# Low halves a unit later, output banks held out of the round, the values' activation right behind the taps

## The reference

```
x, 256 x 1024
first block
  h = rmsnorm(x);  proj = h @ w_in                       (1024 x 3592)
  mixer 1: q, k, v of 4 heads of 128 through a causal convolution of 4 taps and silu,
           then the gated delta rule in chunks of 64 (a triangular solve per chunk and a scan),
           rmsnorm, times silu(z)
           and differential attention, 4 heads, two maps each: softmax a - lam * softmax b
  x = x + [rule, attention] @ w_out
  x = x + (silu(gate) * up) @ w_down,  d_ff 2816;  final rmsnorm
second block
  mod = silu(c) @ w_ada + b_ada                          (1024 x 6144, one row)
  mixer 2: attention of 8 heads of 64 with a relative bias, and glu -> depthwise convolution
           of 31 taps -> layer norm -> silu; both projected, gated and mixed by w_mix_o
  x = x + (gelu(gate) * value) @ w_down, with a convolution of 3 taps ahead of the gelu
```

## Time and profile before

| | us |
|---|---|
| median of 3 runs (794.73 to 796.6) | 796.13 |
| the profiled execution | 794.25 |
| its span, first to last instruction | 792.4 |
| TensorE busy | 754.2 (95%) |
| VectorE busy | 575.6 (73%) |
| ScalarE busy | 390.8 (49%) |
| GpSimd busy | 27.8 (4%) |
| mean granted TensorE clock | 0.988 of full |

### The profile page before, as it was taken

One profiled execution on the slowest core, in us unless ns is written; L12 is line 12 of the kernel. 1 busy time (PEld: TensorE's weight loads), 2 busy tenths in 40 slices (PEclk: granted clock), 3 DMA queues, 4 the chain that ended last, 5 costly groups with the idle time before them and its releaser, 6 DMA issues.

```text
span 792.4 us, 13350 instructions
## 1 busy us (share of the span) xinstructions
PE 754.2 (95%) x5290; PEld 694.6 (88%) x5290; DVE 575.6 (73%) x963; ACT 390.8 (49%) x661; POOL 27.8 (4%) x32
## 2 busy tenths in 40 slices
PE   7998999678999999999999989999999999999996
PEld 7987999677799999999979987799979899999995
DVE  5748888655665867768668998867766766766776
ACT  5472222644543534434565434458256655655644
POOL 0030000010000000000013000000000000000000
PEclk9999999889999999999999999999999999999999
DMA  7834444432279888789815632354444665465531
GB/s 289 281 94 157 134 160 159 157 110 81 80 242 403 324 299 285 271 282 335 306 55 186 212 108 73 114 213 142 155 157 135 212 196 202 161 193 204 161 134 53
DMA packets 40526, 148.94 MB, mean 188 GB/s; under 512 B 4496, under 2 KB 4624, under 8 KB 40080
## 3 DMA queue, kind: packets, MB, share of 16 engines
q1 hardware_dynamic: 39600, 142.91, 52.5%
q10 hardware_dynamic: 864, 5.18, 1.7%
HBM read 147.02 MB, written 1.05 MB: 187 GB/s over the span
## 4 chain that ended last, share of the span: by engine, by line
PE 76%; DVE 12%; ACT 7%; issue 3%; DMA 1%; POOL 0%; DVEq 0%; SPq 0%; ACTq 0%
PE bank L1014 13%; PE bank L1017 13%; PE bank L1015 13%; PE bank L1055 6%; PE bank L1053 6%; PE bank L1056 6%; PE bank L1031 5%; PE bank L1180 5%; DVE wlo L1410 3%; PE bank L1044 3%; DVE arena L1416 3%; ACT whi L1956 2%; ACT arena L1956 2%; DVE arena L1410 2%; ACT XN L1956 1%
## 5 line engine op out<-in xcount | busy, mean ns | idle before, releaser
L1014 PE MATMUL bank<-hh,whi 128*128 128x256 f32 x1008 | 289.6, 287 | 0.8 <-DVE hl L1410 0.5
L1015 PE MATMUL bank<-hl,whi 128*128 128x256 f32 x1008 | 285.9, 284 | 0.0
L1017 PE MATMUL bank<-hh,wlo 128*128 128x256 f32 x1008 | 285.8, 284 | 0.0
L1410 DVE TENSOR_TENSOR wlo<-raw,whi 128x1024 fp32r<-128x1024 f32 x202 | 243.1, 1236 | 48.6 <-ACT whi L1956 48.5
L1956 ACT ACTIVATE whi<-raw 128x1024 fp32r<-128x1024 f32 x202 | 202.4, 1047 | 27.9 <-DMA raw<-w_dram 20.0
L1014 PEld LDWEIGHTS bank<-hh,whi 128*128 128x128 f32 x1008 | 194.0, 192 | 5.0 <-issue 2.9
L1015 PEld LDWEIGHTS bank<-hl,whi 128*128 128x128 f32 x1008 | 193.9, 192 | 1.5
L1017 PEld LDWEIGHTS bank<-hh,wlo 128*128 128x128 f32 x1008 | 193.9, 192 | 0.0
L1416 DVE SCALAR_TENSOR_TENSOR arena<-bank,cols,arena 128x255 f32<-128x255 f32 (+3 forms) x138 | 58.9, 480 | 33.6 <-ACT arena L1956 31.8
L1956 ACT ACTIVATE arena<-bank 128x256 f32<-128x256 f32 (+2 forms) x65 | 26.9, 422 | 96.3 <-PE bank L1017 71.2
L1055 PE MATMUL bank<-wlo,fh 128*128 128x512 f32 x176 | 69.2, 393 | 1.1 <-DVE wlo L1410 1.1
(11 more groups left out here) (169 smaller groups left out, 888.6 us busy)
## 6 DMA issues: line engine op xcount, KB each, us to landing
raw<-w_dram SPq DMA_DIRECT2D x268, 512.0 KB, 4.7
arena<-rows_dram ACTq DMA_DIRECT2D x1, 1792.0 KB, 10.2
X<-x_dram SPq DMA_DIRECT2D x2, 512.0 KB, 4.3
arena<-rows_dram ACTq DMA_DIRECT2D x1, 1024.0 KB, 13.6
arena<-bias_dram ACTq DMA_DIRECT2D x1, 1024.0 KB, 16.9
out_dram<-X SPq DMA_DIRECT2D x4, 256.0 KB, 2.0
const<-const_dram ACTq DMA_DIRECT2D x1, 640.0 KB, 3.8
arena<-bias_dram ACTq DMA_DIRECT2D x1, 512.0 KB, 6.1
```

The costliest lines, as they stand in the source:

```text
L1014: e.matmul(o, a, hh[:, k, :], start=(k == 0), stop=False)
L1015: e.matmul(o, a, hl[:, k, :], start=False, stop=False)
L1017: ins = e.matmul(o, wlo[:, s, k * 128:k * 128 + 128], hh[:, k, :], start=False, stop=(k == 7))
L1410: return e.tensor_tensor(out, a, b, op)
```

## The change

Six edits:
1. In the early stream two a units fewer per early main unit: the sixteen of them follow main units 16 to 27 (two behind 18, 20, 22 and 24), where they followed 14 to 27 (two behind 19 and 23).
2. `prepare` splits in two steps. `hi` (ScalarE) is placed at once; `prep` (VectorE's low half or ada product, SyncE's fetch) is placed one call later while `lag` is on, that is during the turns of both mixers.
3. `silu` 2 follows directly on conv 10. The flag that lets `vturn` go is set one turn sooner, and `delta` has one turn more ahead of it, so that `vturn` keeps its place.
4. The banks of o0 and o1 are taken with a hold, dropped when `la_rows` 1 is placed; `silu` 3 moves from behind `turn_la` to ahead of `la_rows` 1.
5. `turn1` 4 goes ahead of `scores1` 5.
6. The two subtractions ident - Ym move on VectorE from `lev_first` to the end of `lev_mask`.

```diff
@@ stream
-        for _ in range((14 <= n < 28) + (n in (19, 23))):
+        for _ in range((16 <= n < 28) + (n in (18, 20, 22, 24))):
@@ Plan
+        self.lag, self.late = False, []
     def prepare(self, last):
+        new = []
         while self.prepared <= last:
...
                 self.lo_on[i] = (sem, self.lo_count[sem])
+                self.step("hi", i)
+            new.append(i)
+            self.prepared += 1
+        for i in self.late + ([] if self.lag else new):
             self.step("prep", i)
-            self.prepared += 1
+        self.late = new if self.lag else []
@@ main1
             P.step("conv", f)
+            if f == 10:
+                P.step("silu", 2)
             yield
-        last = qk(3)
-        next(last)
-        yield
-        P.step("silu", 2)
         flags.add("v")
-        yield from last
+        yield from qk(3)
@@ delta
         while "v" not in flags:
             yield
+        yield
...
-        P.fill("o0")
+        held = [P.take(hold=True)]
+        P.fill("o0", held[0])
         P.step("values_la", 0)
...
-        P.fill("o1")
+        held.append(P.take(hold=True))
+        P.fill("o1", held[1])
         P.step("values_la", 1)
         P.step("la_rows", 0)
         yield
         P.step("la_sums", 1)
         yield
-        P.step("la_rows", 1)
-        yield
         while "s7" not in flags or ("z", 0) not in flags:
             yield
+        P.step("silu", 3)
+        P.step("la_rows", 1)
+        P.held.difference_update(held)
+        yield
         held = P.take(hold=True)
         P.fill("oT0")
         P.fill("oT1", held)
         P.step("turn_la")
-        P.step("silu", 3)
@@ attention1
+                if n == 5:
+                    P.fill(f"pt1{n - 1}")
+                    P.step("turn1", n - 1)
                 for m in range(2):
                     P.fill(f"s1{n}{m}")
...
-            if n:
+            if n and n != 5:
                 P.fill(f"pt1{n - 1}")
@@ both mixers
+    P.lag = True
     turns(...)
+    P.lag = False
@@ VectorE
-            def lev_first():
                 for b in range(2):
                     w.wait_ge("ym", b + 1)
                     tt(Um[:, b, :, :], rep(K("ident"), 4), Ym[:, b, :, :], ALU.subtract).then_inc(sems["um0"], 1)
+
+            def lev_first():
@@ ScalarE
-            def prep(i):
-                if i in place:
-                    ...
+            def hi(i):
+                ...
```

More of the change, by code:

```diff
@@ L1959, in start @@
                 e.dma_start(const[:, 0, :], const_d[:, 0, :]).then_inc(sems["const"], 16)
-            def prep(i):
-                if i in place:
[L1963 to L1967, removed]
+            def hi(i):
+                s, n = place[i] % HL, place[i]
+                w.wait_ge(*fetched(i))
+                if n >= HL:
+                    w.wait_ge(*P.done[P.split[n - HL]])
+                af(whi[:, s, :], raw[:, i % RAW, :], ACT.Copy).then_inc(sems["hi"], 1)
             def sumsq(q):
@@ L2273, in _ @@
             does = {
-                "start": start, "prep": prep, "square": sumsq, "squares": sumsq, "sumsq": sumsq, "root": root, "rows": rows, "tv": tv, "th": th, "split_ba": split_ba,
+                "start": start, "hi": hi, "square": sumsq, "squares": sumsq, "sumsq": sumsq, "root": root, "rows": rows, "tv": tv, "th": th, "split_ba": split_ba,
                 "conv": conv, "silu": silu, "lam": lam_, "vd": vd_, "qk": qk, "z": z, "gates": gates, "dsq": dsq, "decay": decay,
```

## The result

The changed kernel takes 786.36 us (median of 4 runs, 786.13 to 787.85) beside 795.86 for the kernel before (4 runs, 794.73 to 796.6). The ratio is 0.9886, interval 0.9868 to 0.9903: 1.1% faster. The forecast was 785.2, in a range of 778.5 to 792.5.

The account below looks back on a forecast made before the run. TensorE bounds the kernel, so time lies only in its waits and the low clock behind them. Terms 4.1 + 4.3 + 1.8 - 0.8 + 1.5 = 10.9 us off 794.25 give 783.3, median 785.2, range 778.5 to 792.5.

Parts of the forecast that it names:

- Part 1: First mixer, before the first level: later low halves and moved ada units shorten TensorE's 3.38 us wait; 4.1 us gained.
- all three go: VectorE ahead of T at the first level: ada product of 0.75 us, wait of 0.75 and ada product of 1.28 disappear.
- Part 2: Behind conv 10: values' Silu right behind the taps removes the 5.95 us wait before v's transposes; net 4.3 us gained.
- the ring: Six raw weight buffers, main units 16 to 24: later release makes some fetches late for ScalarE's high halves; -0.8 us.
- -1.0 for a copy and +0.8 for the wait of 2.11 us: Behind solve 0: solution's copy behind later exps loses 1.0 us; ada product replacing the wait before 167.25 gains 0.8.
- Part 3: End of first mixer: z's earlier activation removes most of the 1.98 us wait before 180.37; 1.8 us gained, hold 0.
- Rival A: Values 6: its bank wait goes too and TensorE is next held by turn 7; 782.0 us, chance 0.12.
- B: Conv 10 to output scaling: moved ada products on VectorE eat the gain; 790.6 us, chance 0.22.
- C: Calls 16 to 24: late raw buffer release delays ScalarE 2.4 us each, kernel slower; 806.0 us, chance 0.08.
- D: w_out's heads, 180 to 216 us: saved time returns as waits; 796.1 us, about the old time, chance 0.07.
- Second mixer: 446 to 471 us and the last projections: VectorE's lead from the lag gives net 1.5 us.
- +2.1 for the waits of 1.09 and 1.03 us, -0.6 for the late low half: Second mixer: VectorE's 2.1 us lead covers waits before 462.63 and 471.18; a low half behind u2 costs 0.6.

Follow-up runs that it names:

- the second measurement: The changed kernel run once more, nothing altered: 787.19 us, ratio 0.9893 to the kernel before.
- the flushes: Changed kernel with late low halves placed at once ahead of `spread_od` in the rule and ahead of u2 in the second mixer: 784.33 us, ratio 0.9859.
- the longer hold: Changed kernel with the hold of the output banks dropped one turn later, so values 6 gets bank 5 instead of 4: 783.61 us, ratio 0.9845.

## Why the prediction was right, and where it was not

**Part 1, 4.1 us: the size right, its two edits not told apart.** The forecast was a restart at 68.5; 69.88 less the start's 1.46 is 68.4, with a full clock behind it, 4.07 us sooner at the next main product. The step "all three go" is right for the two edits together. But I explained the products of 0.75 and 1.28 us by edit 1 and gave the lag only the wait of 0.75 between them. The lag alone gives 3.8 of the 4.1 us: it takes the wait away and also puts the product of 1.28 us behind T. All the other edits without the lag, the moved products among them, give 1.0, below my lower bound of 2.0 for "only the two products go": a product ahead of a wait costs nothing as far as it only fills time that would else be waited. On top of the lag the moved products give 0.3.

**Part 2 with the ring, 4.3 - 0.8 = 3.5 us.** The Silu stands behind the taps, the table load is hidden, the new waits on TensorE are 3.28 and 0.65 us (2.8 and 1.1 forecast), the high half waits 0.72 us for its fetch (0.9 forecast). Solve 0 gained 8.10 - 4.07 = 4.0 us (4.5 less the ring's 0.8 forecast), values 6 3.6. That 5.95 us of wait and a low clock were worth 4 and not 7.7 came from following VectorE's queue: two products and a low half stand in front of the scaling of v, as forecast. Behind solve 0 I had -1.0 for a copy and +0.8 for the wait of 2.11 us; -0.4 came of it. The wait is gone (the low half at 165.92 starts with no wait), and the 1.0 stands in no row and was not looked at by itself.

The profiles show what no single term said, that the activation and the lag need each other. How many us sooner than in the kernel before, the start taken out:

| kernel | next main product | from there to values 6 |
|---|---|---|
| lag alone | 3.8 | 0.15 |
| all but the lag | 1.0 | 0.7 |
| all but the activation (edit 3) | 4.1 | 1.25 |
| all but the moved ada units (edit 1) | 3.8 | 4.7 |
| all (the changed kernel) | 4.1 | 3.6 |

With the lag alone the transposes of v still wait 6.36 us. Without the lag the other edits bring solve 0 2.7 us nearer, but VectorE then stands 1.16 and 2.11 us for high halves, and 0.7 are left at values 6. Each row is one profile.

The page that puts a table switch at 2.66 us (the Trainium skill, "ScalarE: Activation LUTs", What ACT_TABLE_LOAD costs) is not borne out here: the load takes 1.28 us and the exp starts 1.30 us after the load's start (137.26 and 138.56).

**Part 3, 1.8 us.** The wait before the heads' weights is 0.41 us instead of 1.98, so 1.6 for z's activation. From values 6 to these weights the gain is 2.3 us, because the low clock behind values 6 was milder (0.60 over 3.84 us is 1.5 lost, 0.52 over 4.73 was 2.3). These 0.7 us are luck: the changed kernel's two profiles have 0.60 and 0.59 over those 3.84 us, six other profiles with the same wait of 3.8 us have 0.50. The count of the round was right: the hold changes nothing, since values 6 gets bank 4 with it and without. Rival A's mechanism exists but needs the hold one turn longer.

**Rivals B, C and D.** B (the moved products eat the gain) did not happen as a whole, but its mechanism is there: by the table above they make the way from the first level to values 6 1.1 us longer (3.6 gained against 4.7). C did not happen: TensorE was busy 46.78 of 46.79 us between 73.31 and 120.10, and ScalarE waited for a fetch 1.6 us in all between 100 and 170. D did not happen as a whole, but a piece of it did, at w_out.

**Second mixer, 1.5 us: the failed term.** The step "+2.1 for the waits of 1.09 and 1.03 us, -0.6 for the late low half" gave 1.5 in its first part (the shift grows from 8.93 to 10.46; a wait of 0.62 us stays) and was wrong in its second. I weighed the late low half against the moment at which TensorE asks and found 0.6 us; the wait is 0.36, but it is a second stop 0.5 us behind the one of 1.32, and in this profile the clock then falls. Of the 10.46 us 0.5 is lost in small pieces ahead of these projections, 0.4 with this wait and 1.7 with the clock (4.00 us at 0.57, below), 2.6 in all. Net of the lag in this mixer -1.1 us in this profile, where I had +1.5. Where the clock stays full, as in the profile without a hold, it is +0.4 (575.27 us from the first main product behind w_out to the end, against 575.67 without the lag in this mixer). The forecast term was too high either way.

**What no term had: w_out.** The lag queues low halves behind the first heads, as it does behind u2, and TensorE waited 0.87 us for one; VectorE of the changed kernel there:

```profile
189.07 0.69 DVE L1426 TENSOR_TENSOR ml<-arena,mh 128x512 fp32r<-128x512 f32 x1 [0.70 <-ACT mh L1972]
189.68 4.62 DVE L1426 TENSOR_TENSOR wlo<-raw,whi 128x1024 fp32r<-128x1024 f32 x4
```

Four low halves in a row, the first of which TensorE needed at 190.1. I checked this for u2 and not for the heads, where the same list is used.

**The sum.** Forecast 10.9; the profile without its start gives 7.8, the medians 9.5 and, in the second measurement, 8.4. The misses are 1.0 at w_out and 2.6 in the second mixer, against 0.5 more in part 3. Where the clock does not fall in the last projections, as in four of the seven profiles with both waits there, the loss is 1.7 less; where it is 0.50 behind values 6, as in six of eight, 0.7 more. The forecast was too high by 3.1 us by the profile and by 1.4 and 2.5 by the medians. What was missing lies at w_out and in the second mixer; up to the heads' weights the first mixer's 9.4 (4.1 + 3.5 + 1.8) came out as 9.9, of which 0.7 are luck.

## What to carry to other kernels

A queue that makes one engine wait for another's fresh result is better relaxed for all its entries at once than cleared of some work: look at what the waiting engine does between the request and the use, since a piece of work that stands ahead of a wait may cost nothing. Edits that bring little by themselves can bring much together, as the lag and the other edits did between the first level and values 6 (0.15 and 0.7 us alone, 3.6 together), so an edit is to be taken out of the whole as well as put in alone. But such a lag has to be closed at every place where the consumer comes straight behind a chain on the same engine; find those places before, by walking the queue of the delayed engine at each stage's end. And a hold of a buffer must last until the next claimant has been dealt one: one turn decided about 3 us here.

## What the runs showed of the hardware

The clock behind one and the same pair of stops was not always the same. Seven profiles have the waits of 1.32 and 0.36 us in the last projections, with the same instructions around them. In three (the changed kernel twice, the lag alone) the granted clock of the next 4 us is 0.57 to 0.60, in four it is 1.00. Two of them, the changed kernel and the one without a hold, in the table of stretches:

```profile
539.62:540.48 0.86, 0.50 (x2) 0.29 (x2) 0.86 (x2) 0.86 (x2) 0.00 (x0) 1.00 0.00 0
540.48:544.48 4.00, 4.00 (x21) 4.00 (x22) 4.00 (x5) 2.37 (x3) 0.00 (x0) 0.57 0.63 179
```

```profile
539.70:543.70 4.00, 4.00 (x33) 4.00 (x34) 4.00 (x6) 3.39 (x4) 0.00 (x0) 1.00 0.64 199
```

21 matmuls in the one and 33 in the other, in the same 4.00 us. The four profiles with the wait of 1.32 us alone (the kernel before, without the lag in one mixer or both, with the flushes) have full clock there. So the same instructions with the same stops were followed by a granted clock of about half in some executions and not in others; what decides between them these runs do not show. In these projections it fell only where the second stop was there, but three of seven profiles against none of four are too few to show that the stop of 0.36 us is the cause. The mean clock of whole runs points the same way: the four runs with the longer hold have 0.996, 0.992, 0.992 and 0.996, and all nine runs of the two kernels without either stop have 0.996. Behind the wait of 3.8 us before values 6 the clock fell in all eight profiles that have it: over the next 3.84 us to 0.60 and 0.59 in the changed kernel's two and to 0.50 in the others; behind the one of 1.98 us before turn 7 it stayed at 1.00 in all three.
